# Seven block products for the value half of the up projections, on one Trainium2 core

## The chip, the core and the metric

The kernel runs on one core of one Trainium2 chip. The metric is the device time of the whole program in microseconds. Engines: PE (TensorE, matmul), PEld (its weight load), DVE (VectorE), ACT (ScalarE), POOL (GpSimd), SP (SyncE, which issues the loads; SPq is its queue). The SBUF and PSUM memories are shared by the engines; semaphores order them.

## What is computed

Two decoder layers for a prompt of 512 tokens and 8 x 8 sample tokens, 576 tokens in all, kept as `xT[128, 8, 576]` (features on partitions). Layer 0 mixes tokens with an mLSTM, layer 1 with sliding-window attention. Each is followed by the part that the change touches:

```
def conv_glu(h, conv_buf, w_up, conv_w, conv_b, w_down):   # h = rmsnorm(x)
    up = h @ w_up                     # 1024 -> 2 * 2816
    g, u = up[..., :D_FF], up[..., D_FF:]
    gp = jnp.concatenate([conv_buf, g], axis=1)
    gc = conv_b + sum(conv_w[j] * gp[:, j:j + T] for j in range(3))
    y = (gelu(gc) * u) @ w_down       # 2816 -> 1024
    return y, gp[:, T:]
```

`g` is called the gate half, `u` the value half. Weights are float32. Each is split into a high and a low float16 part; a product is three float16 matmuls (high x high, high x low, low x high; `THREE`).

## The kernel before

**Up projection** (`up0`, `up1`, one for each layer). 22 tiles of 128 outputs for either half, worked in pairs of tiles: pair i holds tiles i and i + 11. Its four units come in the order gate i, value i, gate i + 11, value i + 11. A unit is 8 k-blocks x 3 x 2 token halves of 288 (`HALF`) = 48 matmuls (`fm_unit`, L426), so a pair is 192. The weights pass through a ring of four slots: SP loads 512 KB into `stage` (`load`, L2234) once the DVE has read what was there; ACT writes the high part `wH` (`split_act`, L294), the DVE the low part `wL` (`split_dve`, L300), each once for each unit, and PE reads both. Behind each gate unit the DVE scales PSUM into `G` (L712), ACT and the DVE do the three taps of the convolution (L635, L716, L720) and ACT the gelu (L642); behind the value unit the DVE scales and multiplies (L729, L733). Sums of the quarters of the pair (L739 to L746, `tmix`) and their high and low parts (`hidH`, `hidL`, L647 to L651, L753 to L759) prepare the down projection. The order on each engine is written out by hand in `act_ffn` and `dve_ffn`, as a loop over i; only semaphores tie the engines together.

**Down projection** (`down0`, `down1`). It already uses a seven-product scheme (Winograd's form of Strassen's): for each of four pairs of output tiles the weight is cut into quarters A11, A12, A21, A22 (`quart`, 704 KB each), and seven products of sums of quarters with sums of hidden quarters replace eight. A product is 11 x 3 = 33 matmuls of 288 columns (L544), a pair 231, a layer 924. The sums of weights are made by the DVE (`weight_sum`, L365, L369) and by two adding DMAs on the POOL queue (`pool_sums`, `add_a22`, L377). The high part comes from ACT (`block_high`, L348), the low one from the DVE (`block_low`, L354). Each product goes to a PSUM bank of its own or adds to one; the DVE adds them into `xT` (`add_block`, L408).

## Time and profile before

| | us |
|---|---|
| median of 3 runs | 1230.67 (1230.65 to 1231.26) |
| the profiled execution, whole | 1233.18 |
| its span | 1231.4 |
| PE busy | 1212.6 (98%) |
| DVE busy | 808.1 (66%) |
| ACT busy | 536.9 (44%) |
| PE chain in one up projection after its first unit | 252.84 |
| PE chain in one down projection | 113.20 |

The profile is of one execution. The whole time is 1.8 us more than the span, and the profiled execution is 2.5 us above the median. A row of the timeline gives start, duration, engine, line and operands; durations of independent neighbours on one engine overlap a little, so starts can be closer than a duration.

### The profile page before, as it was taken

The page shows a single profiled execution, that of the slowest core. Times are in us where ns is not written, and L with a number is a line of the kernel's source. Part 1 is how long each engine was busy: PE and PEld are TensorE (multiplying, and loading weights), DVE is VectorE, ACT ScalarE, POOL GpSimd, SP SyncE. Part 2 cuts the span into 40 slices and gives each one's busy share as a digit, 9 for nine tenths or more (in the row PEclk, how much of TensorE's full clock was granted, in tenths as well). Part 3 has the DMA queues.
Part 4 walks back from the last instruction along what each step waited for, and adds up shares of the span by engine and source line. Part 5 has one row for each costly group of instructions (what it writes and reads, how often), then busy time and mean ns, then how long its engine had stood idle before and what let it go on. Part 6 is the DMA issues. An engine that isn't in the chain of part 4 may idle for free.

```text
span 1231.4 us, 24687 instructions
## 1 busy us (share of the span) xinstructions
PE 1212.6 (98%) x9846; PEld 921.9 (75%) x9846; DVE 808.1 (66%) x1309; ACT 536.9 (44%) x849; POOL 81.2 (7%) x227
## 2 busy tenths in 40 slices
PE   7999999999999999999999999999999999999998
PEld 6855777777777777777774456777777777778886
DVE  5644566566767767776763479755777677777564
ACT  6322355345434434443344459744344344333332
POOL 1000010000000000000003200000000000000010
PEclk9999999999999999999999999999999999999999
DMA  8642243233332232345646220022322323515672
GB/s 214 236 104 75 63 146 108 74 105 96 89 87 85 85 102 85 111 123 148 154 117 221 81 69 2 2 69 86 103 85 85 95 80 97 156 47 136 152 177 56
DMA packets 188830, 129.58 MB, mean 105 GB/s; under 512 B 4929, under 2 KB 177851, under 8 KB 188690
## 3 DMA queue, kind: packets, MB, share of 16 engines
q1 hardware_dynamic: 181562, 101.80, 28.6%
q0 software_dynamic: 7200, 26.80, 8.3%
q8 instruction: 51, 0.84, 0.3%
q14 instruction: 17, 0.14, 0.1%
HBM read 109.15 MB, written 9.86 MB: 97 GB/s over the span
## 4 chain that ended last, share of the span: by engine, by line
PE 94%; DVE 3%; SPq 1%; ACT 1%; DMA 1%; issue 0%; DVEq 0%
PE PS L426 57%; PE PS L544 18%; PE PS L442 10%; SPq L2234 1%; PE PS L1155 1%; PE PS L1175 1%; DMA rowsF<-in_ffn_conv_b 1%; PE PS L1130 1%; DVE P L2184 1%; DVE st L2165 1%; PE PS L1373 1%; PE PS L1406 1%; ACT P L1692 1%; PE PS L1229 0%; PE PS L1158 0%
## 5 line engine op out<-in xcount | busy, mean ns | idle before, releaser
L426 PE MATMUL PS<-zH,wH 128*128 128x288 f16 x1408 | 287.6, 286 | 0.0
L426 PE MATMUL PS<-zL,wH 128*128 128x288 f16 x1408 | 287.6, 286 | 0.0
L426 PE MATMUL PS<-zH,wL 128*128 128x288 f16 x1408 | 287.6, 286 | 0.0
L544 PE MATMUL PS<-hidH,blk 128*128 128x288 f16 x1232 | 227.9, 286 | 0.0
L300 DVE SCALAR_TENSOR_TENSOR wL<-stage,wH 128x1024 f16<-128x1024 f32 x140 | 170.3, 1219 | 56.9 <-ACT wH L294 56.9
L294 ACT ACTIVATE wH<-stage 128x1024 f16<-128x1024 f32 x140 | 146.4, 1048 | 131.7 <-PE PS L426 65.5
L544 PE MATMUL PS<-hidL,blk 128*128 128x288 f16 x616 | 176.2, 286 | 0.0
L426 PEld LDWEIGHTS PS<-zH,wH 128*128 128x128 f16 x1408 | 137.8, 98 | 35.0
L426 PEld LDWEIGHTS PS<-zL,wH 128*128 128x128 f16 x1408 | 137.8, 98 | 34.7
L426 PEld LDWEIGHTS PS<-zH,wL 128*128 128x128 f16 x1408 | 137.8, 98 | 34.7
L544 PEld LDWEIGHTS PS<-hidH,blk 128*128 128x128 f16 x1232 | 120.5, 98 | 30.2
L635 ACT ACTIVATE acc<-G,pff 128x592 f32<-128x592 f32 x44 | 38.7, 881 | 161.2 <-DVE G L712 161.2
L426 PE MATMUL PS<-hnH,wH 128*128 128x288 f16 x396 | 81.6, 288 | 1.8 <-issue 1.2
L426 PE MATMUL PS<-hnL,wH 128*128 128x288 f16 x396 | 81.7, 288 | 0.0
L426 PE MATMUL PS<-hnH,wL 128*128 128x288 f16 x396 | 81.5, 288 | 0.0
L712 DVE SCALAR_TENSOR_TENSOR G<-PS,three 128x288 f32<-128x288 f32 x132 | 39.0, 351 | 55.3 <-PE PS L426 46.0
L716 DVE SCALAR_TENSOR_TENSOR acc<-G,pff,acc 128x592 f32<-128x592 f32 x44 | 36.7, 835 | 55.9 <-ACT acc L635 55.9
L544 PEld LDWEIGHTS PS<-hidL,blk 128*128 128x128 f16 x616 | 60.3, 98 | 15.1
L354 DVE SCALAR_TENSOR_TENSOR blk<-quart,blk 128x1408 f16<-128x1408 f32 x32 | 51.7, 1617 | 25.5 <-ACT blk L348 25.5
L348 ACT ACTIVATE blk<-quart 128x1408 f16<-128x1408 f32 x32 | 43.0, 1368 | 52.2 <-DMA quart<-quart 34.2
L348 ACT ACTIVATE blk<-mixed 128x1408 f16<-128x1408 f32 x24 | 33.0, 1374 | 60.0 <-DVE mixed L365 37.8
L408 DVE SCALAR_TENSOR_TENSOR xT<-PS,xT 128x288 f32<-128x288 f32 (+1 forms) x56 | 30.2, 540 | 37.6 <-PE PS L544 37.6
(383 smaller groups left out, 1746.4 us busy)
## 6 DMA issues: line engine op xcount, KB each, us to landing
...
quart<-in_w_ffn_down SPq DMA_DIRECT2D x32, 704.0 KB, 5.0
...
quart<-quart POOLq DMA_DIRECT2D x8, 704.0 KB, 6.8
mixed<-quart POOLq DMA_DIRECT2D x8, 704.0 KB, 7.9
...
```

What stands on the lines that cost most here:

```text
L294: nc.scalar.activation(wH[:, slot, :], stage[:, slot, :], ACT.Copy, scale=WSCALE).then_inc(hi_ready, 1)
L300: nc.vector.scalar_tensor_tensor(out=wL[:, slot, :], in0=stage[:, slot, :], scalar=WSCALE, in1=wH[:, slot, :], op0=ALU.mult, op1=ALU.subtr ...
L348: nc.scalar.activation(blk[:, g % RING, 0, :], WEIGHT[j], ACT.Copy, scale=WSCALE).then_inc(hi_ready, 1)
L354: nc.vector.scalar_tensor_tensor(out=blk[:, g % RING, 1, :], in0=WEIGHT[g % BLOCKS], scalar=WSCALE, in1=blk[:, g % RING, 0, :], op0=ALU.mu ...
L408: nc.vector.scalar_tensor_tensor(out=x, in0=ps, scalar=1.0 / WSCALE, in1=x, op0=ALU.mult, op1=ALU.add).then_inc(added, 1)
L426: m = nc.tensor.matmul(out[:, hf, :], w[a][:, slot, 128 * (at + j):128 * (at + j + 1)], xs(b, k)[:, HALF * hf:HALF * (hf + 1)], start=(fir ...
L442: m = nc.tensor.matmul(out, x, w[:, cols], start=first, stop=last, skip_group_check=True)
L544: m = nc.tensor.matmul(down_bank(g), blk[:, g % RING, a, 128 * k:128 * (k + 1)], (hidH, hidL)[b][:, HIDDEN[j], k, :], start=(k == 0 and (a ...
L635: nc.scalar.activation(acc[:, s, 0:CC], G[:, s, 2:GC], ACT.Identity, bias=pff[:, k, 38 + L:39 + L], scale=pff[:, k, 32 + 3 * L + 2:33 + 3 ...
L712: last = nc.vector.scalar_tensor_tensor(out=out, in0=a, scalar=1.0 / WSCALE, in1=b, op0=ALU.mult, op1=ALU.mult)
L716: nc.vector.scalar_tensor_tensor(out=acc[:, s, 0:CC], in0=G[:, s, 0:CC], scalar=pff[:, k, 32 + 3 * L:33 + 3 * L], in1=acc[:, s, 0:CC], op0 ...
L1130: nc.tensor.matmul(PS[:, 4 + i % 2, 0:DV + 1], kw[:, i, 128 * h:128 * (h + 1)], vM[:, i, h, :], start=True, stop=True).then_inc(hsem["u"], 1)
```

## The change

**Up projection.** The first and the last pair (0 and 10) stay as they were. For pairs 1 to 9 the gate units stay, but the two value units become seven products of 4 x 3 = 12 matmuls of 288 columns (`product_of`), 84 where there were 96. The two tiles are the two output halves, k-blocks 0 to 3 and 4 to 7 the two input halves, the token halves the two column halves. Their weight tiles are v0 (tile i, slot 1 of `stage`) and v1 (tile i + 11, slot 3). The weight sums are made in place: S1 in slot 3 by an adding DMA of 256 KB (`step_s1`), N2 in slot 1 by the DVE (`up_n2`), then S4 and S3 in slot 1 by two more adding DMAs, one after the other (`step_s4`, `step_s3`, both in slot 1). The high and low parts of N2, S3 and S4 go to `sH` and `sL`. The sums of the inputs (`tH`, `tL`) are made once for each layer behind the mixer's output projection (`pair_scaled`, `t_sums`, `t_high`, `t_low`) and brought home by two DMAs. Four products of a pair gather in one PSUM bank; after each ACT copies the bank (`keep`: p1, u2, u3, c21) to `val`, and the DVE adds the other banks (`value`: c11, c22, c12). Gelu now writes into `h32`, and one DVE instruction multiplies (`hidden`). The loops and orders of all five queues in `pe_ffn`, `act_ffn`, `dve_ffn`, `pool_ffn` and the SP's `ffn` are rewritten; the peeled first and last steps included.

Units of a step on PE in order: u1, u2 (from v0), u3 (v1), u4 (N2), u5 (gate i, 48 matmuls), u6 (S3), half of gate i + 11, u7 (v1), u8 (S4), the other half (u9 is its end).

**Down projection.** Same count of products and matmuls, another order. Products 0, 2, 4 and 6 share one bank; ACT copies it after products 0, 2 and 4 (`keep_block`); the DVE combines in `val`, scales by `rstd` and adds (`combine_blocks`). One sum that a DMA made (into `mixed`) is now made by the DVE (`weight_s3`), one by a DMA (`pool_s4`).

Core of the diff (the deleted bodies of `two`, `weight_sum`, `pool_sums` and `add_block` can be seen above):

```diff
+        QUARTERS = ((A21, 1, 0), (A11, 0, 0), (A12, 0, 1), (A22, 1, 1))
+        N2_OF, S3_OF = 1, 2
+
+        WEIGHT = (quart[:, A11, :], quart[:, A12, :], mixed[:, :], quart[:, A21, :], quart[:, A11, :],
+                  quart[:, A12, :], quart[:, A22, :])
+        HIDDEN = (0, 2, 5, 3, 4, 1, 6)
+        BANK = (0, 3, 0, 2, 0, 1, 0)
+        OPENS = (0, 1, 3, 5)
...
+        def up_high(act, L, i, what):
+
+            j = i + 1
+            whole = what in ("g0", "g1") or (isinstance(j, int) and j == KH - 1)
+            first = isinstance(i, int) and i == 0
+            if what == "v1" and not whole:
+                act.wait_ge(s1_landed, up_s(L, j))
+            split_act(act, up_unit(L, j, what), up_base(L, i) + (SLOT[what] + 1 if first else FREED[what]),
+                      1 if whole else 2)
+
...
+        def s34_high(act, L, i):
+
+            j = i + 1
+            act.wait_ge(s3_landed, 16 * (len(MIXED) * L + j))
+            if not (isinstance(i, int) and i == 0):
+                act.wait_ge(unit_used, up_base(L, i) + FREED["s34"])
+            nc.scalar.activation(sH[:, WQ:3 * WQ], stage[:, 1, :], ACT.Copy, scale=WSCALE).then_inc(hi_ready, 2)
...
+        def s34_low(dve, L, j):
+
+            dve.wait_ge(hi_ready, up_base(L, j) + LOW["s34"])
+            nc.vector.scalar_tensor_tensor(out=sL[:, WQ:3 * WQ], in0=stage[:, 1, :], scalar=WSCALE,
+                                           in1=sH[:, WQ:3 * WQ], op0=ALU.mult, op1=ALU.subtract).then_inc(lo_ready, 2)
...
+        def up_n2(dve, L, j):
+
+            dve.wait_ge(s1_landed, up_s(L, j))
+            dve.wait_ge(lo_ready, up_base(L, j) + LOW["v0"])
+            nc.vector.tensor_tensor(stage[:, 1, 0:WQ], stage[:, 1, 0:WQ], stage[:, 3, 0:WQ],
+                                    ALU.subtract).then_inc(sums, 1)
...
+        def keep_block(act, L, g):
...
+            act.wait_ge(unit_used, block_num(L, g) + 1)
+            row, a = {0: (0, HALF), 2: (0, 0), 4: (1, 0)}[j]
+            nc.scalar.activation(val[row][:, a:a + HALF], down_bank(g), ACT.Copy).then_inc(ff["copied"], 1)
...
+        def combine_blocks(dve, L, g):
+
+            p, j = divmod(g, BLOCKS)
+            n0 = ADDS * L + PAIR_ADDS * p
+            last = p == PAIRS - 1
+            if j in (0, 2):
+                return
...
+            if j == 1:
+                dve.wait_ge(ff["copied"], kept(L, p) + 1)
+                sum_of(dve, v01, v01, b3, ALU.add, added)
+            elif j == 3:
+                dve.wait_ge(ff["copied"], kept(L, p) + 2)
+                sum_of(dve, v00, v00, b2, ALU.subtract, added)
+            elif j == 4:
+                dve.wait_ge(ff["copied"], kept(L, p) + 3)
+                sum_of(dve, v10, v10, b2, ALU.subtract, added)
+                dve.wait_ge(added, n0 + 3)
+                scale_row(dve, 0, HALF, 1)
+                if last:
+                    dve.wait_ge(added, n0 + 4)
+                    add_row(dve, 2 * p + 1, 0, HALF, 1)
+            elif j == 5:
+                n = n0 + (6 if last else 5)
+                dve.wait_ge(added, n0 + 2)
+                sum_of(dve, v00, v00, b1, ALU.add, added)
+                dve.wait_ge(added, n)
+                scale_row(dve, 0, T, 0)
+                dve.wait_ge(added, n + 1)
+                add_row(dve, 2 * p, 0, T, 0)
             else:
-                q = (0, 3, 3, None, 2, 0, 1)[j]
-                x = two[:, HALF * q:HALF * (q + 1)]
-            nc.vector.scalar_tensor_tensor(out=x, in0=ps, scalar=1.0 / WSCALE, in1=x, op0=ALU.mult,
...
+        def t_sums(dve, L, k):
...
+            n0 = 2 * (4 * L + k)
+            nc.vector.tensor_tensor(tt4[:, 0, :], zz[:, 0, :], zz[:, 1, :], ALU.subtract).then_inc(turned_x["t"], 1)
+            nc.vector.tensor_tensor(tt4[:, 1, :], zz[:, 2, :], zz[:, 0, :], ALU.subtract)
+            dve.wait_ge(turned_x["t"], n0 + 1)
+            nc.vector.tensor_tensor(tt4[:, 2, :], tt4[:, 0, :], zz[:, 2, :], ALU.subtract).then_inc(turned_x["t"], 1)
+            dve.wait_ge(turned_x["t"], n0 + 2)
+            nc.vector.tensor_tensor(tt4[:, 3, :], zz[:, 3, :], tt4[:, 2, :], ALU.add).then_inc(turned_x["sum"], 1)
...
+            def step(i):
+                n, vb, cb = up_base(L, i), VALS * L + 3 * i, COPIES * L + 4 * i - 2
+                pe.wait_ge(lo_ready, n + LOW["v0"])
+                pe.wait_ge(copied, cb)
+                product_of(v0, 0, x_quarter(0, 1), 0, True)
+                pe.wait_ge(vals, vb)
+                product_of(v0, WQ, x_quarter(1, 1), 3, True)
+                pe.wait_ge(lo_ready, n + LOW["v1"])
+                product_of(v1, 0, x_turned_pair(0), 2, True)
+                pe.wait_ge(copied, cb + 1)
+                product_of(of_sums, 0, x_turned_pair(2), 0, False)
+                pe.wait_ge(ff["gate"], KF * L + 2 * i + 1)
+                whole(i, 0, 0)
+                pe.wait_ge(lo_ready, n + LOW["s34"])
+                pe.wait_ge(copied, cb + 2)
+                product_of(of_sums, WQ, x_turned_pair(1), 0, False)
+                pe.wait_ge(ff["gate"], KF * L + 2 * i + 2)
+                whole(i, 1, 0, ks=range(KQ))
+                pe.wait_ge(copied, cb + 3)
+                product_of(v1, WQ, x_turned_pair(3), 0, False)
+                pe.wait_ge(vals, vb + 2)
+                product_of(of_sums, 2 * WQ, x_quarter(1, 0), 2, False)
+                whole(i, 1, 0, ks=range(KQ, KD))
+
...
+            def step_first(i):
+                keep(i, "p1")
+                up_high(act, L, i - 1, "g1")
+
+            def step_mid(i):
+                hidden_raw(i - 1)
+                keep(i, "u2")
+                hidden_turned(i - 1)
+                s34_high(act, L, i - 1)
+                tap(i, 0)
+                keep(i, "u3")
+
+            def step_last(i):
+                up_high(act, L, i, "v0")
+                gelu(i, 0)
+                n2_high(act, L, i)
+                keep(i, "c21")
+                up_high(act, L, i, "v1")
+                up_high(act, L, i, "g0")
...
+            def step_first(i):
+                value(i, "c11")
+                up_low(dve, L, i, "g1")
+                hidden(i - 1, 1)
+                turned(i - 1)
+                hidden_lows(i - 1)
+                s34_low(dve, L, i)
+                gate(i, 0)
+
+            def step_last(i):
+                up_low(dve, L, i + 1, "v0")
+                conv(i, 0)
+                value(i, "c22")
+                up_n2(dve, L, i + 1)
+                n2_low(dve, L, i + 1)
+                value(i, "c12")
+                up_low(dve, L, i + 1, "v1")
+                hidden(i, 0)
...
+            def step_s1(j):
+                pool.wait_ge(staged[3], (TURN0[f"up{L}"] + j + 1) * 16)
+                pool.dma_start(stage[:, 3, 0:WQ], stage[:, 3, WQ:2 * WQ], accum_op=ALU.add).then_inc(s1_landed, 16)
+
+            def step_s4(j):
+
+                pool.wait_ge(sums, up_sum(L, j))
+                pool.dma_start(stage[:, 1, WQ:2 * WQ], stage[:, 1, 0:WQ], accum_op=ALU.add).then_inc(s4_landed, 16)
+
+            def step_s3(j):
+
+                pool.wait_ge(s4_landed, up_s(L, j))
+                pool.wait_ge(lo_ready, up_base(L, j) + LOW["n2"])
+                pool.dma_start(stage[:, 1, 0:WQ], stage[:, 3, WQ:2 * WQ], accum_op=ALU.add).then_inc(s3_landed, 16)
+
...
+                    up_load(1, u)
+                for i in range(2, KH):
+                    for what in ("g0", "g1", "v1", "v0"):
+                        if what == "v1":
+                            sp.wait_ge(s3_landed, 16 * (len(MIXED) * L + i - 1))
+                            sp.wait_ge(lo_ready, up_base(L, i - 1) + LOW["v1"])
+                        else:
+                            sp.wait_ge(lo_ready, up_base(L, i - 1) + LOW["s34" if what == "v0" else what])
+                        up_load(i, SLOT[what])```

The DVE in the first layer's up projection, where a pair follows another. Before (one half of a loop pass; wL<-stage is `split_dve`, G<-PS the scaling of a gate unit, ntmp is `h32`):

```order
L720 SCALAR_TENSOR_TENSOR acc<-G,pff,acc 128x592
L299 REGISTER_ALU
L300 SCALAR_TENSOR_TENSOR wL<-stage,wH 128x1024 [waits hi_ready]
L727 REGISTER_ALU
L729 SCALAR_TENSOR_TENSOR ntmp<-PS,three 128x576 [waits ffn0_hL,unit_used]
L731 REGISTER_ALU
L733 TENSOR_TENSOR ntmp<-ntmp,acc 128x512 [waits ffn0_gelu,ffn0_u]
L734 TENSOR_TENSOR ntmp<-ntmp,acc 128x64
L739 TENSOR_TENSOR three<-ntmp 128x288 [waits ffn0_h32]
L299 REGISTER_ALU
L300 SCALAR_TENSOR_TENSOR wL<-stage,wH 128x1024 [waits hi_ready]
```

Now, from `s34_low(1)` to `hidden(1, 0)` (L466 is `s34_low`, L473 `up_n2`, L452 `n2_low`, L519 `value`, L1088 `hidden`):

```order
L466 SCALAR_TENSOR_TENSOR hidL<-stage,hidH 128x1024 [waits hi_ready]
L1058 SCALAR_TENSOR_TENSOR G<-PS,three 128x512 [waits unit_used,ffn_hist]
L1060 SCALAR_TENSOR_TENSOR G<-PS,three 128x8x8
L341 SCALAR_TENSOR_TENSOR wL<-stage,wH 128x1024 [waits hi_ready]
L1070 SCALAR_TENSOR_TENSOR acc<-G,pff,acc 128x592 [waits ffn_acc]
L1074 SCALAR_TENSOR_TENSOR acc<-G,pff,acc 128x592 [waits ffn_half]
L519 TENSOR_TENSOR C<-C,PS 128x288 [waits ffn_copied,unit_used]
L473 TENSOR_TENSOR stage<-stage 128x512 [waits lo_ready,s1_landed]
L452 SCALAR_TENSOR_TENSOR hidL<-stage,hidH 128x512 [waits hi_ready]
L519 TENSOR_TENSOR val<-val,PS 128x288 [waits unit_used]
L341 SCALAR_TENSOR_TENSOR wL<-stage,wH 128x1024 [waits hi_ready]
L1088 SCALAR_TENSOR_TENSOR ntmp<-val,ntmp 128x576 [waits ffn_gelu,ffn_vals]
```

What moved: the low part of the next pair's v0 (the first L341) now stands two instructions behind the read of slot 1 by L466, and the convolution, the sums and the multiplication of the pair stand behind it.

SP at the same place, before (one of four loads in a pass) and now (two pairs of tiles):

```order
L2234 ISA [waits lo_ready]
L2234 DMA stage<-in_w_ffn_up 128x8x128
L2233 REGISTER_ALU
L2234 ISA [waits lo_ready]
L2234 DMA stage<-in_w_ffn_up 128x8x128
```

```order
L2720 DMA stage<-in_w_ffn_up 128x8x128 [waits lo_ready] x6
L2720 DMA stage<-in_w_ffn_up 128x8x128 [waits lo_ready,s3_landed]
L2720 DMA stage<-in_w_ffn_up 128x8x128 [waits lo_ready] x3
L2720 DMA stage<-in_w_ffn_up 128x8x128 [waits lo_ready,s3_landed]
L2720 DMA stage<-in_w_ffn_up 128x8x128 [waits lo_ready] x3
```

What moved: before, each load waited for the low part of the unit that had its slot. Now the load of v0 comes last of its four and waits for the low parts of S3 and S4; that of v1 waits for the landing of S3.

ACT in pair 1, from the high part of S3 and S4 to that of pair 2's v1 (L335 is the high part of a tile, L447 that of N2, L461 that of S3 and S4, L942 `keep`, L908 the tap, L916 the gelu):

```order
L461 ACTIVATE hidH<-stage 128x1024 [waits s3_landed]
L908 ACTIVATE acc<-G,pff 128x592 [waits ffn_gate]
L942 ACTIVATE C<-PS 128x288 [waits unit_used,ffn_h32]
L335 ACTIVATE wH<-stage 128x1024 [waits unit_used,staged1]
L916 ACTIVATE ntmp<-acc 128x512 [waits hidden_low,ffn_conv]
L917 ACTIVATE ntmp<-acc 128x64
L447 ACTIVATE hidH<-stage 128x512 [waits unit_used,weight_sums]
L942 ACTIVATE C<-PS 128x288 [waits unit_used]
L335 ACTIVATE wH<-stage 128x1024 [waits staged3,unit_used,s1_landed]
```

What moved: before, taps, high parts, gelu and the copies to `hidH` alternated for each tile. Now the copies of PSUM banks stand among them, the high part of v0 stands ahead of the gelu, that of N2 behind it.

## Rows read from the trace of the kernel before

**Rows 1.** The page: span, and PE (busy us, share, instructions).
```profile
span 1231.4 us, 24687 instructions
PE 1212.6 (98%) x9846; PEld 921.9 (75%) x9846; DVE 808.1 (66%) x1309; ACT 536.9 (44%) x849; POOL 81.2 (7%) x227
```
**Rows 2.** The chain that ended last: start us, us, what; up0, down0.
```profile
283.43 252.84 PE PS L426 x2064
536.27 113.20 PE PS L544 x924
```
**Rows 3.** Windows: us, busy us (instructions) by engine, clock, DMA; up projection, attention.
```profile
380.00:403.50 23.50, 23.50 (x194) 18.77 (x193) 16.73 (x28) 9.43 (x12) 1.07 (x6) 1.00 0.31 89
727.00:760.00 33.00, 30.21 (x270) 20.23 (x269) 30.99 (x78) 29.55 (x105) 0.00 (x0) 1.00 0.01 4
```
**Rows 4.** Timeline of the DVE in up0: start us, us, instruction, idle before, releaser.
```profile
381.46 1.22 DVE L300 SCALAR_TENSOR_TENSOR wL<-stage,wH 128x1024 f16<-128x1024 f32 x1
...
391.51 0.83 DVE L716 SCALAR_TENSOR_TENSOR acc<-G,pff,acc 128x592 f32<-128x592 f32 x1 [1.32 <-ACT acc L635]
392.50 0.84 DVE L720 SCALAR_TENSOR_TENSOR acc<-G,pff,acc 128x592 f32<-128x592 f32 x1 [0.16 <-DVE acc L716]
...
395.98 0.69 DVE L733 TENSOR_TENSOR ntmp<-ntmp,acc 128x512 f32<-128x512 f32 x1
...
397.21 0.45 DVE L744 TENSOR_TENSOR three<-ntmp 128x288 f32<-128x288 f32 x1
...
399.09 0.75 DVE L756 TENSOR_TENSOR hidL<-ntmp,hidH 128x576 f32 x1
399.76 1.35 DVE L759 TENSOR_TENSOR hidL<-three,hidH 128x1152 f32 x1
401.06 0.89 DVE L712 SCALAR_TENSOR_TENSOR G<-PS,three 128x288 f32<-128x288 f32 x3
```
**Rows 5.** Timeline of ACT there.
```profile
385.18 0.44 ACT L647 ACTIVATE hidH<-ntmp 128x288 f32 x1 [0.69 <-DVE ntmp L734]
390.45 0.88 ACT L635 ACTIVATE acc<-G,pff 128x592 f32<-128x592 f32 x1 [4.83 <-DVE G L712]
391.23 1.04 ACT L294 ACTIVATE wH<-stage 128x1024 f16<-128x1024 f32 x1
393.37 0.70 ACT L642 ACTIVATE acc<-acc 128x592 f32<-128x592 f32 x1 [1.10 <-DVE acc L720]
...
398.16 1.16 ACT L651 ACTIVATE hidH<-three 128x1152 f32 x1 [0.55 <-DVE three L746]
```
**Rows 6.** Timeline of SP's queue there, and landing of `stage` loads, 380 to 430.
```profile
382.84 16.86 SPq L2234 DMA_DIRECT2D stage<-in_w_ffn_up  x4
DMA to landing us min/median/max: 3.6/3.7/4.2
```
**Rows 7.** DMA issues, whole run: out<-in, queue, count, KB each, median us to landing.
```profile
quart<-in_w_ffn_down SPq DMA_DIRECT2D x32, 704.0 KB, 5.0
quart<-quart POOLq DMA_DIRECT2D x8, 704.0 KB, 6.8
mixed<-quart POOLq DMA_DIRECT2D x8, 704.0 KB, 7.9
...
out_sample_k<-qtok POOLq DMA_DIRECT2D x8, 8.0 KB, 2.0
```
**Rows 8.** Timeline in down0: an adding DMA's issue, and the copy that waits for it.
```profile
617.30 0.86 POOL L377 DMA_DIRECT2D quart<-quart  x1 [24.62 <-DVE mixed L365]
622.65 1.38 ACT L348 ACTIVATE blk<-quart 128x1408 f16<-128x1408 f32 x1 [3.25 <-DMA quart<-quart]
```
**Rows 9.** Timeline of the DVE, last unit of the mixer's output projection.
```profile
276.73 0.76 DVE L474 SCALAR_TENSOR_TENSOR xT<-PS,xT 128x576 f32 x1 [1.43 <-PE PS L426]
278.55 0.82 DVE L487 SCALAR_TENSOR_TENSOR zL<-xT,pd,zH  x1 [1.07 <-ACT zH L480]
```
**Rows 10.** Timeline at the end, the last add into xT.
```profile
1226.49 0.46 DVE L408 SCALAR_TENSOR_TENSOR xT<-PS,xT 128x288 f32<-128x288 f32 x1 [4.13 <-PE PS L544]
```

More of the change, by code:

```diff
@@ L766, in dve_ffn @@
+            hidden_lows(i)
+            block_low(dve, L, 0)
+            weight_n2(dve, L, 0)
+            i = KH - 1
+            gate(i, 0)
+            conv(i, 0)
+            hidden(i, 0)
+            gate(i, 1)
+            conv(i, 1)
+            block_low(dve, L, 1)
+            hidden(i, 1)
+            turned(i)
+            hidden_lows(i)
+            block_work(dve, L, 2)
             if L == 0:
@@ L1488, in _ @@
             act.sem_inc(free["qkv"], TT)
[L1489 to L1490 removed]
+            act.sem_inc(ff["gate"], 2)
             act.wait_ge(dI, 16)
```

730 lines of the change are left out of this document (479 added, 251 removed).

## The prediction

> **What bounds the kernel now.** The page comes first: PE is busy 1212.6 of 1231.4 us [rows 1]. Then the chain of waits: each layer's up projection is one piece of PE without another engine in it, 2064 matmuls in 252.84 us, and the down projection 924 in 113.20 us [rows 2]. Both give 0.1225 us for a matmul of 288 columns. A pair of tiles takes 192 of them, 23.52 us; the window of a pair has PE busy throughout, the DVE for 16.73 and ACT for 9.43 of 23.50 us [rows 3]. So removed matmuls count in full as long as nobody becomes late, and the DVE has 6.8 us to spare in a pair. The timelines of the DVE and ACT then give the length of each step [rows 4, 5]: DVE 0.45 us for 288 columns, 0.69 for 512, 0.75 for 576, 1.22 for 1024, 1.35 for 1152; ACT 0.44 for 288, 1.04 for 1024, 1.16 for 1152. Independent neighbours start 0.08 us before the end of the one ahead; a DVE instruction that needs the one ahead starts 0.16 us behind its end.
>
> **Removed.** 9 pairs x 12 matmuls x 2 layers = 216, x 0.1225 = 26.5 us (13.2 a layer). A middle pair would take 180 x 0.1225 = 22.05 us. The down projection keeps its 924.
>
> **Added work in a middle pair.** DVE: the splits of S3, S4 (1.22) and N2 (0.69), N2 itself (0.69) and three additions (3 x 0.45); less in the multiplications. In order without any wait for another engine, with the same-engine waits of 0.16, its instructions from the low part of v0 to that of S3 and S4 take 18.0 us and the gate's 0.8 more: still below 22.05. By busy time alone it fits. ACT has some 13 us. What decides is the order and one slot of `stage`.
>
> **The loop through slot 1.** S3 and S4 of pair i stand in slot 1 until the DVE has read them (`s34_low`). Only then may SP load v0 of pair i + 1 there, and the DVE's next instruction but the gate's two is that tile's low part, with all else of the pair behind it. I follow one round, with 0 at the end of `s34_low(i)`:
> - SP issues 0.16 us later (the DVE ends at 382.68, the issue is at 382.84 [rows 4, 6]); landing after 3.7 [rows 6]: 3.9. ACT's high part 1.04: 4.95. The DVE can start the low part at 5.0; the 0.8 us of `gate(i, 0)` are over long before.
> - Low 1.22, two taps 0.83 and 0.84 with 0.16 between: 7.95. c22 8.3. N2 8.9. ACT's high part of 512 columns, not in the trace, lies between 0.44 and 0.70 us [rows 5]; I take 0.63: 9.6. Low 10.35. c12 10.7. ACT copies c21 and makes v1's high part: 10.9; low 12.15. `hidden(i, 0)` 12.85.
> - PE waits for c22 ahead of u8: 8.4. u8 and half a gate unit are 1.47 + 2.94, the last matmul and the start behind the wait some 0.25: u9 is done at 13.05, and with it `gate(i, 1)` can start. So both ways come to 13.05.
> - From there: gate 0.83, ACT's tap 0.88 with 0.26 ahead and 0.18 behind it, taps on the DVE end at 3.98, c11 4.35, g1's low 5.5, `hidden` 6.2, `turned` (576, 288, 288 columns, each behind the last) 8.3, low of three raw quarters 9.3, ACT's high part of the four sums ends 9.6, their low 10.95, `s34_low` 12.1.
> The round is 13.0 + 12.1 = 25.1 us, 3.05 above PE's own 22.05 and 1.6 above the pair of before. PE stands about 2.5 us ahead of u8 and 0.5 ahead of u6 in each. It does not shrink when PE waits, as PE is only one of its ways. Round one starts in step: `s34_low(1)` ends 0.4 us before PE wants it. Eight rounds follow (pairs 1 to 9): 8 x 3.05 - 0.4 = 24.0 us a layer.
>
> The bounds of a round: without any of the waits for ACT it is 18.0 + 5.1 = 23.1. Upwards, the load shares the DMA engines with S1 of the same pair, issued about then: 4.2, the longest of these loads [rows 6], to 5.0, that of 704 KB [rows 7], makes 25.6 to 26.4. I take 25.1, as the loads of before also had others close by.
>
> **The adding DMAs.** 256 KB is not in the trace: 2.0 us for 8 KB, 5.3 for 704 KB alone (617.30 to 622.65), medians of 6.8 and 7.9 beside loads [rows 7, 8]. I take 4, nearer to 704 KB's than its size. S4 and S3 one after the other have 13.5 us from N2 to `s34_high`, and with the load of v1 and S1 the whole ring closes up to 6.7 us each. So they are hidden, at a price of zero; the cover is gone above 6.7. The Trainium skill (DMA: Bandwidth & Descriptors, Anatomy of one DMA) states a fixed 2.0 us and bytes at 436 GB/s for this path, 2.6 us here; for 704 KB it would say 3.7, less than the 5.3 of the trace. By either the sums stay hidden.
>
> **Start of the up projection.** In the last four units of the mixer's projection the DVE gets `t_sums` (four of 0.45, two waits) and `t_low` (1.35) on top of 3.5 us; a unit is 5.88 and the DVE's part becomes 7.4 from the second on. It is 3.3 us late at the last. There zL came at 279.37 [rows 9], and its matmuls at 276.6 + 7 x 0.735 = 281.7: 2.3 us of cover. PE waits 1.0 us. Pair 9 has another order (g0 ahead of v0): c22 ends at 6.6 and u8 is 0.9 late.
>
> **Seam to the down projection.** Pair 10 gives PE 23.5 us of cover, but the DVE comes with a pair's debt. From `s34_low(9)` as 0: PE ends pair 10 at 34.4. The DVE: v0's low part 9.6, `gate(9, 1)` 11.4, lows of pair 9 25.8, `block_low(0)` (1.62 as in the trace's blocks) 27.3, `weight_n2` 29.8 (quarters landed by 22, their DMA sum by 28), `gate(10, 0)`, taps and `hidden` 35.9, `gate(10, 1)` and taps 39.8, `block_low(1)` 41.3, `hidden`, sums and lows 46.8, `block_low(2)` 48.3. PE waits for the value copy (0.9), for block 1 (2.4), for the last lows (1.7) and for block 2 (0.7): 5.7 us. Before, this place cost nothing [rows 2]. Bounds 2 and 10.
>
> **Down projection.** DVE work stays near 22 of 28.3 us a pair. The new dependence is A22, loaded last: `block_low(6)` ends at 18.3 of a pair, load 5.0, S1 5.3 to 6.8, N2 1.6, high 1.4, low 1.6: 33.6 to 35.1, wanted at 28.3 + 8.1 = 36.4. Bank copies have a whole product (4.04) each. Nothing. At each layer's end, the last block needs a scaling and an addition where one addition of 0.46 was [rows 10]: 0.6 us.
>
> **Sum** against the profiled execution: per layer -13.2 + 24.0 + 1.0 + 0.9 + 5.7 + 0.6 = +19.0. Two layers: +38. Span 1269, whole 1271; against the median 1230.67 it is 1268.7, rounded to 1268.
>
> **Rivals.**
> - *PE keeps its rate in the steps* (the load is early enough, or the DVE's steps overlap more than its timeline shows): -26.5 + 2 x (1.0 + 5.7 + 0.6) = -11.9, 1219 us. For it: DVE and ACT have the busy time. Against: the wait on slot 1 is a plain semaphore, and the low part stands first in an in-order queue. With the round at its lower bound of 23.1: 16 x 1.05 instead of 48 gives 1237. Faster than before is decided at a round below about 22.7.
> - *The adding DMAs close the ring* (6.7 us is the point): at 7.9 each, the median beside loads [rows 7], three of them add 3.6 us a round, 16 x 3.6 = 58: 1326. Against: a third of the bytes.
> - *The clock.* PE now stands 3 of 25 us. It kept its upper level, 2.4 GHz (granted 1.00), in the attention with 30.21 of 33.00 us busy [rows 3]. If it went to 1.2 GHz behind each wait for a quarter of a pair's matmuls, 5.5 us a round, it would be some 1356. The Trainium skill (TensorE: Matmul & The Clock Gate, Part 1) says that idling gates the clock; the attention's row speaks against it for gaps of this size.
>
> **Chances.** Forecast (1245 to 1290) 0.70; lower-bound round (about 1237) 0.10; PE at its rate (1219) 0.11; ring of DMAs or clock 0.09. A measurement can tell 0.2%, 2.5 us. Faster 0.12, same 0.03, slower 0.85. The range leaves out the 1219 and the upper rivals: 1235 to 1298.
>
> **What would show it.** The chain would no longer be PE alone in the up projections: loads of `stage`, ACT wH and DVE wL in it, starts of `s34_low` 25 us apart, 22 if I am wrong. PE idle ahead of u8 released by the DVE's c22, and ahead of block 1 at the seam. ACT's wait for `stage` slot 1 some 2 us a round. Wrong would be: a longer or shorter landing of the 512 KB load (16 rounds: 0.5 us is 8 us in all), adding DMAs above 6.7 us, or DVE instructions on `val` and `stage` that differ from rows of the same width.

## The result and the profile after

The changed kernel takes 1321.56 us (median of 4 runs, 1317.62 to 1322.12), the kernel before 1230.66 (4 runs, 1230.58 to 1231.26): a ratio of 1.0731, 95% interval 1.071 to 1.0752. It is slower, as forecast, but by 90.9 us where I had 38; the range ended at 1298. The profiled execution of the changed kernel took 1317.62 us in all, its span is 1315.8, 84.4 above the 1231.4 of before.

The page of the changed kernel, its first rows, the shares of the chain by engine, and the group of u8's first matmuls (section 5: busy us, mean ns of one, idle us ahead of them and what ended it):

```profile
span 1315.8 us, 24171 instructions
## 1 busy us (share of the span) xinstructions
PE 1216.3 (92%) x9630; PEld 907.9 (69%) x9630; DVE 864.7 (66%) x1299; ACT 615.1 (47%) x1035; POOL 150.1 (11%) x285
...
PE 53%; DVE 18%; ACT 9%; issue 9%; DMA 8%; SPq 1%; DVEq 1%; ACTq 0%; POOL 0%; POOLq 0%
...
L757 PE MATMUL PS<-zH,hidH 128*128 128x288 f16 x72 | 29.3, 407 | 50.7 <-DVE C L519 50.7
```

216 matmuls are gone (9846 to 9630), worth 26.5 us at 0.1225 each, and yet PE is busy 3.7 us longer than before [rows 1]. It stands idle 99.5 us of its span, where it stood 18.8. Half of that is one place: ahead of u8, until the DVE has made c22 (L519). And u8's matmuls, 286 ns each in the rest of the up projection, take 407 there.

The chain of waits of the changed kernel through one round (pair 3 to 4; start us, us, what), answering to [rows 2], in which such a round was PE alone:

```profile
396.02 1.23 DVE hidL L466
397.26 4.37 DMA stage<-in_w_ffn_up
401.79 1.06 ACT wH L335
402.95 0.11 DVE wL L341
...
405.83 0.46 DVE C L519
406.34 3.06 PE PS L757 x12
409.40 3.17 PE PS L601 x24
412.60 0.06 DVE G L1058
```

PE's idle time there and its first matmul of u8 and of u9 (timeline), then the granted clock around them (windows: us, busy us (instructions) for PE, PEld, DVE, ACT, POOL, then PE's clock, DMA share, GB/s), answering to [rows 3]:

```profile
406.34 0.42 PE L757 MATMUL PS<-zH,hidH 128*128 128x288 f16 x1 [3.00 <-DVE C L519]
...
412.39 0.29 PE L757 MATMUL PS<-zH,wH 128*128 128x288 f16 x1
```

```profile
396.02:423.25 27.23, 24.02 (x182) 18.17 (x181) 18.38 (x26) 12.06 (x18) 4.57 (x9) 0.94 0.44 106
404.00:406.00 2.00, 0.00 (x0) 0.00 (x0) 1.84 (x4) 0.05 (x1) 0.00 (x0) 1.00 0.00 0
406.00:408.00 2.00, 1.66 (x8) 1.04 (x9) 1.30 (x3) 1.81 (x5) 1.02 (x2) 0.57 0.00 0
408.00:410.00 2.00, 2.00 (x11) 1.33 (x10) 0.83 (x3) 1.74 (x2) 0.04 (x1) 0.57 0.72 131
```

The ring is the one of the forecast, link for link: `s34_low` (L466), the load of v0 into slot 1, ACT's high part, the DVE's low part, the taps, c22, u8, half a gate unit, `gate`. Its round is 27.3 us and not 25.1: `s34_low` starts at 315.57, 341.45, 368.74, 396.02, 423.25, 450.54, 477.84, 505.24 and 532.12 in layer 0, and 216.6 us apart from first to last in layer 1 too. Behind 3.00 us without a matmul the granted clock stands at 0.57, near the lower level of 1.2 GHz, and the 36 matmuls from u8 on take 6.05 us (406.34 to 412.39) instead of 4.42.

Three more places, PE's timeline at each (start of the up projections, layer 1's convolution rows, end of layer 0's down projection), then the chain ahead of the first and the adding DMAs of the whole run (DMA issues: count, KB each, median us to landing):

```profile
304.54 0.42 PE L757 MATMUL PS<-zH,wH 128*128 128x288 f16 x1 [6.09 <-ACT C L934]
919.00 0.42 PE L757 MATMUL PS<-zH,wH 128*128 128x288 f16 x1 [8.27 <-ACT C L934]
...
1190.01 2.03 PE L833 MATMUL PS<-C,convO 128*99 128x128 f32 x8 [7.27 <-POOL convO L1240]
...
688.07 0.39 PE L617 MATMUL PS<-wH,zH 128*128 128x512 f16 x1 [3.58 <-DVE wL L341]
```

```profile
287.41 0.53 POOL tL L1266
287.95 8.75 DMA stage<-stage
```

```profile
stage<-stage POOLq DMA_DIRECT2D x54, 256.0 KB, 3.2
```

### The profile page after: what moved, and what is told of

The parts are those of the page before. It is cut to its first block, busy times and chain, and to the rows that moved or that the text cites. A ratio compares the mean times of both kernels' runs of the same rounds, so it can differ in the third digit from the quotient of the medians.

```text
span 1315.8 us, 24171 instructions
## 1 busy us (share of the span) xinstructions
PE 1216.3 (92%) x9630; PEld 907.9 (69%) x9630; DVE 864.7 (66%) x1299; ACT 615.1 (47%) x1035; POOL 150.1 (11%) x285
## 3 DMA queue, kind: packets, MB, share of 16 engines
q0 software_dynamic: 15552, 45.68, 15.6%
## 4 chain that ended last, share of the span: by engine, by line
PE 53%; DVE 18%; ACT 9%; issue 9%; DMA 8%; SPq 1%; DVEq 1%; ACTq 0%; POOL 0%; POOLq 0%
PE PS L601 15%; PE PS L820 15%; PE PS L617 9%; PE PS L757 6%; DMA stage<-in_w_ffn_up 5%; DVE acc L1070 2%; ACT wH L335 2%; DVE wL L341 2%; DVE hidL L466 1%; DMA stage<-stage 1%; ACT acc L908 1%; ACT hidH L461 1%; DVE three L1097 1%; DVE ntmp L1088 1%; PE PS L1617 1%
## 5 line engine op out<-in xcount | busy, mean ns | idle before, releaser
L341 DVE SCALAR_TENSOR_TENSOR wL<-stage,wH 128x1024 f16<-128x1024 f32 x140 | 170.6, 1221 | 168.1 <-ACT wH L335 167.6
L335 ACT ACTIVATE wH<-stage 128x1024 f16<-128x1024 f32 x140 | 144.7, 1047 | 132.7 <-PE PS L617 58.8
L601 PE MATMUL PS<-zH,wH 128*128 128x288 f16 x832 | 171.7, 288 | 0.7 <-DVE zL L662 0.7
L601 PE MATMUL PS<-zL,wH 128*128 128x288 f16 x832 | 170.0, 286 | 0.0
L601 PE MATMUL PS<-zH,wL 128*128 128x288 f16 x832 | 169.9, 286 | 0.0
L908 ACT ACTIVATE acc<-G,pff 128x592 f32<-128x592 f32 x44 | 38.8, 881 | 128.9 <-DVE G L1060 128.9
L601 PEld LDWEIGHTS PS<-zH,wH 128*128 128x128 f16 x832 | 82.4, 99 | 23.6 <-DVE zL L662 1.3
L601 PEld LDWEIGHTS PS<-zL,wH 128*128 128x128 f16 x832 | 81.9, 98 | 21.3
L601 PEld LDWEIGHTS PS<-zH,wL 128*128 128x128 f16 x832 | 81.4, 98 | 20.5
L601 PE MATMUL PS<-hnH,wH 128*128 128x288 f16 x396 | 80.9, 286 | 1.8 <-issue 1.2
L601 PE MATMUL PS<-hnH,wL 128*128 128x288 f16 x396 | 80.8, 286 | 0.0
L601 PE MATMUL PS<-hnL,wH 128*128 128x288 f16 x396 | 80.8, 286 | 0.0
L412 DVE SCALAR_TENSOR_TENSOR blk<-quart,blk 128x1408 f16<-128x1408 f32 x48 | 77.5, 1618 | 0.8 <-ACT blk L406 0.7
L757 PE MATMUL PS<-zH,hidH 128*128 128x288 f16 x72 | 29.3, 407 | 50.7 <-DVE C L519 50.7
L916 ACT ACTIVATE ntmp<-acc 128x512 f32<-128x512 f32 x44 | 27.8, 631 | 89.0 <-DVE acc L1074 89.0
L519 DVE TENSOR_TENSOR val<-val,PS 128x288 f32<-128x288 f32 x60 | 27.1, 451 | 55.9 <-PE PS L820 29.6
L757 PE MATMUL PS<-zH,wH 128*128 128x288 f16 x144 | 42.4, 295 | 14.4 <-ACT C L934 14.4
## 6 DMA issues: line engine op xcount, KB each, us to landing
quart<-in_w_ffn_down SPq DMA_DIRECT2D x32, 704.0 KB, 5.6
stage<-stage POOLq DMA_DIRECT2D x54, 256.0 KB, 3.2
quart<-quart POOLq DMA_DIRECT2D x8, 704.0 KB, 5.7
quart<-mixed POOLq DMA_DIRECT2D x8, 704.0 KB, 5.3
```

What stands on the lines that cost most here:

```text
L335: nc.scalar.activation(wH[:, slot, :], stage[:, slot, :], ACT.Copy, scale=WSCALE).then_inc(hi_ready, inc)
L341: nc.vector.scalar_tensor_tensor(out=wL[:, slot, :], in0=stage[:, slot, :], scalar=WSCALE, in1=wH[:, slot, :], op0=ALU.mult, op1=ALU.subtr ...
L412: nc.vector.scalar_tensor_tensor(out=blk[:, g % RING, 1, :], in0=WEIGHT[g % BLOCKS], scalar=WSCALE, in1=blk[:, g % RING, 0, :], op0=ALU.mu ...
L519: nc.vector.tensor_tensor(out, a, b, op).then_inc(done, 1)
L601: m = nc.tensor.matmul(out[:, hf, :], w[a][:, slot, 128 * (at + j):128 * (at + j + 1)], xs(b, k)[:, HALF * hf:HALF * (hf + 1)], start=(fir ...
L757: m = nc.tensor.matmul(up_psum(bank), w[a][:, at + 128 * k:at + 128 * (k + 1)], x(b, k), start=(start and k == 0 and (a, b) == THREE[0]), ...
```

## The experiments

The theory after the result, **A**: PE waits for the ring through slot 1, and what the forecast lacked is (1) some 0.6 us more for load and issue, (2) the low clock behind the wait, 1.6 us a round, and (3) two things that GpSimd's queue holds back. The rivals: **B**, the adding DMAs set the round; **C**, the matmuls of u8 are slow for a reason of their own.

### e1_conv_first: c22 ahead of the low part of v0

```diff
@@ ACT, step_last(i)
-                up_high(act, L, i, "v0")
                 gelu(i, 0)
+                up_high(act, L, i, "v0")
...
@@ DVE, step_last(i)
-                up_low(dve, L, i + 1, "v0")
                 conv(i, 0)
                 value(i, "c22")
+                up_low(dve, L, i + 1, "v0")
```

> In the last third of a middle round DVE makes the conv and the copy c22 before the low half of v0's split, and ACT makes gelu(i,0) before its high half; nothing else changes. Theory A (the loop through slot 1, made dearer by TensorE's clock): c22 is then there at about 4.4 us after s34_low instead of 9.0, before TensorE comes to u8 at about 5.9, so the 3.0 us wait ahead of u8 goes, its 12 matmuls take 1.47 us again instead of 3.06, and a round falls from 27.3 to 23.1 to 23.4 us: 16 rounds by 4, about -60 us, time 1255 to 1265. Rival B (the adding DMAs of the quarter sums or their queue on GpSimd set the round): the round stays at 27.0 to 27.5 us and only the place of the wait moves, time 1310 to 1325. Rival C (the wait goes but the low clock has another cause, such as the load of the whole program): round 24.8 to 25.4, time 1280 to 1295.

Measured: 1263.53 us (1260.16 to 1264.98), 1.0261 of before (1.0232 to 1.029). Rounds of 23.4 to 23.9, most 23.43. The DVE's timeline of a round, and u8's group:

```profile
387.12 1.22 DVE L466 SCALAR_TENSOR_TENSOR hidL<-stage,hidH 128x1024 f16<-128x1024 f32 x1
...
391.35 0.83 DVE L1074 SCALAR_TENSOR_TENSOR acc<-G,pff,acc 128x592 f32<-128x592 f32 x1 [0.16 <-DVE acc L1070]
392.10 0.45 DVE L519 TENSOR_TENSOR C<-C,PS 128x288 f32<-128x288 f32 x1
394.06 1.22 DVE L341 SCALAR_TENSOR_TENSOR wL<-stage,wH 128x1024 f16<-128x1024 f32 x1 [1.50 <-ACT wH L335]
```

```profile
L757 PE MATMUL PS<-zH,hidH 128*128 128x288 f16 x72 | 20.6, 286 | 0.7 <-DVE C L519 0.7
```

c22 now ends 4.2 us after `s34_low` and not 9.0, 50.0 of the 50.7 us of idle time ahead of u8 are gone and its matmuls are back at 286 ns. The rounds of both layers, first to last `s34_low`, fell by 28.0 us each: 56 of the 58 us. B and C fall. No work was taken away: only the places of the high and the low part of v0 changed, which now stand behind the gelu on ACT and behind the two taps and c22 on the DVE. But a ring is left, and 23.43 is hardly less than before's 23.52 a pair: PE now waits 1.2 to 1.7 us for `s34_low` in 14 of the rounds. The chain still goes through the load (388.36, 4.19 us), the low part of v0 and all that stands behind it.

### e2b_fill: the waiting time filled with matmuls

```diff
@@ PE, step(i)
                 product_of(v1, WQ, x_turned_pair(3), 0, False)
+                for _ in range(28):
+                    nc.tensor.matmul(PS[:, 1, HALF:512], zH[:, 1, 0:128], zH[:, 0, 0:512 - HALF], start=True, stop=True,
+                                     skip_group_check=True)
                 pe.wait_ge(vals, vb + 2)
```

> TensorE runs 28 matmuls of 224 columns into columns of bank 1 that nobody reads, right ahead of its wait for the copy c22 in every middle pair; they are no part of the computation. By 95 ns each (the rate of the unit matmuls around them at the full clock) they fill 2.66 of the 3.0 us that TensorE stands idle there. Theory A (the idle time lowers TensorE's clock, and the low clock makes u8 3.06 us instead of 1.47): u8 takes about 1.5 us again though the work ahead of it has grown, the round falls from 27.3 to 25.4 to 25.8 us, time 1291 to 1298. Rival B (the clock falls for another reason, for instance by a limit on power): u8 stays near 3 us, the round at 27.3 or above, time 1318 to 1326. Rival C (the 12 matmuls of u8 are slow by what they read or by the bank they write, with the clock only following): u8 stays near 3 us with a granted clock of 1 in its stretch, time 1318 to 1322.

Measured: 1302.94 us (1299.88 to 1303.38), 1.0575 of before (1.0556 to 1.0593): 18.6 us faster than the changed kernel, with 504 matmuls more. PE's timeline at the same place, and the windows:

```profile
402.51 2.85 PE L792 MATMUL PS<-zH 128*128 128x224 f16 x28
405.36 0.30 PE L757 MATMUL PS<-zH,hidH 128*128 128x288 f16 x1
...
409.78 0.29 PE L757 MATMUL PS<-zH,wH 128*128 128x288 f16 x1
```

```profile
404.00:406.00 2.00, 2.00 (x21) 1.62 (x19) 1.80 (x3) 0.84 (x3) 0.20 (x1) 1.00 0.00 0
406.00:408.00 2.00, 2.00 (x19) 1.60 (x17) 1.14 (x3) 2.00 (x4) 0.86 (x1) 1.00 0.22 40
```

The 36 matmuls from u8 on take 4.42 us, the clock is 1.00, and the round is 25.3 to 26.2. So the idle time lowers the clock, and 1.6 us of each slow round is the clock. The time is 5 us above what A gave. A took 1.5 to 1.9 us off all 16 rounds; together they became 21.9 us shorter, and the first of each layer no shorter at all (25.91 and 25.93 us, they were 25.88 and 25.81), since its wait had not lowered the clock. Of the other 3.3 us the profile shows 2.4 ahead of any filling: the 36 matmuls behind the wait at the start of the up projections took 6.60 and 7.25 us, where the changed kernel's took 5.76 and 5.73. `s34_low(1)` of layer 0 starts at 317.61, not 315.57.

### e3_half_load: half of v0's load

```diff
@@ SP, the load of v0 in pairs 2 to 9
+                        if what == "v0" and i < KH - 1:
+                            sp.dma_start(stage[:, 1, 0:WQ]..., tile(i, 1)[:, 0:KQ, :]).then_inc(staged[1], 16)
+                        else:
+                            up_load(i, SLOT[what])
```

> The load of v0 in the middle pairs fetches four of its eight k-blocks, 256 KB instead of 512 KB; half of v0 is left out of the computation and what stands in slot 1 from before is used in its place. Everything else, the order included, is as in the changed kernel. Theory A (the load's landing is a link of the ring s34_low, load, split of v0, c22, u8, gate, s34_low): the load lands 1.0 to 1.8 us earlier than its 4.4 us, and each round is shorter by that and by up to 1.6 us more where the shorter wait ahead of u8 no longer lowers the clock: round 24 to 26.3 us, time 1265 to 1306. Rival B (the ring closes elsewhere, by the adding DMAs on the GpSimd queue): round 27.0 to 27.5, time 1312 to 1324.

Measured: 1292.05 us (1290.76 to 1294.32), 1.0492 of before (1.0468 to 1.0516), 29.5 us less than the changed kernel. The load's piece in the chain is 3.17 us (at 393.88) and not 4.37, so c22 comes 1.2 us earlier; over the 16 rounds the median is 3.57 us where it was 4.57. The rounds now are of two kinds: 24.4 to 25.0 and 26.1 to 26.7. Two of them, PE's first matmul of u8 in each, then two windows of each:

```profile
401.76 0.30 PE L757 MATMUL PS<-zH,hidH 128*128 128x288 f16 x1 [1.79 <-DVE C L519]
...
426.67 0.30 PE L757 MATMUL PS<-zH,hidH 128*128 128x288 f16 x1 [2.30 <-DVE C L519]
```

```profile
402.00:404.00 2.00, 2.00 (x19) 1.59 (x17) 1.30 (x3) 1.81 (x4) 0.86 (x1) 1.00 0.00 0
404.00:406.00 2.00, 2.00 (x19) 1.61 (x17) 1.74 (x3) 1.15 (x2) 0.00 (x0) 1.00 0.72 131
...
426.00:428.00 2.00, 1.33 (x11) 1.07 (x12) 1.30 (x4) 1.54 (x4) 0.69 (x2) 0.97 0.00 0
428.00:430.00 2.00, 2.00 (x10) 1.25 (x9) 1.83 (x3) 2.00 (x3) 0.37 (x1) 0.50 0.61 112
```

The load is on the ring with its full length, and the step between the two kinds is the clock. Of the run's 16 waits ahead of u8 in pairs 1 to 8, the eight up to 1.94 us all have 36 matmuls at full pace behind them (4.42 us); of the eight from 2.14 to 2.45, six have slow ones (5.98 to 6.09).

### e4_pool_order: two moves on GpSimd

```diff
@@ POOL
             history(0, 1)
+            step_s1(1)
             pool.wait_ge(unit_used, SEG0[f"up{L}"])
             for home, new, ready in ((tH, newTH, turned_x["high"]), (tL, newTL, turned_x["low"])):
...
-            step_s1(1)
             tails(0, 0)
...
             pool_s1(pool, L, 0)
-            pool_s4(pool, L, 0)
             tails(KH - 1, 0)
             tails(KH - 1, 1)
+            pool_s4(pool, L, 0)
```

> Two moves in GpSimd's order and nothing else: the sums for pair 1 are issued ahead of the two copies of tH and tL to their home (1.18 MB each), and the two tails of the last row ahead of the second adding DMA of down product 0. Theory (I did not see in the forecast that what is queued ahead on GpSimd delays the start of the up projections and the seam of layer 1): the idle time of TensorE ahead of step 1 (6.1 us in layer 0, 8.3 us in layer 1) falls to under 1.5 us, with it the low clock of u1 and u2 right behind it (1.5 us a layer), and the 7.3 us that TensorE waits in layer 1 for the rows of the convolution falls to under 1.5 us; about -20 us, time 1298 to 1305. Rival (the sums of pair 1 are late by their own loads, and the seam waits for the down weights): both waits stay within 2 us of what they were, time 1312 to 1322.

Measured: 1305.22 us (1303.87 to 1307.85), 1.0609 of before (1.0582 to 1.0636): 16.3 us less than the changed kernel, just short of the 17 to 24 that I had. The 7.27 us wait for the convolution's rows is gone, with 1.50 at the next place. At the start only part went:

```profile
302.28 0.30 PE L757 MATMUL PS<-zH,wH 128*128 128x288 f16 x1 [3.60 <-ACT C L934]
```

3.60 in both layers, not under 1.5. The rest is ACT's own order: the copy of the value bank (L934) stands behind the gelu and a high part. e8 takes that up.

### e5_own_slot: the load taken out of the ring

```diff
+        stageX = sb("stageX", [128, 1024], into=ph)     # over rows 8 and 9 of hidL
...
+        def v0slot(j):
+            return stageX[:, :] if j in (2, 4, 6, 8) else stage[:, 1, :]
...
@@ SP, ahead of the four loads of pair i
+                    if i < KH - 1:
+                        sp.wait_ge(lo_ready, up_base(L, i - 1) + LOW["v0"])
+                        sp.dma_start(v0slot(i)..., tile(i, 1)).then_inc(stagedX if i in (2, 4, 6, 8) else staged[1], 16)
```

> v0 of pairs 2, 4, 6 and 8 has a buffer of its own in rows of the hidden tensor that are not written yet, pairs 3, 5, 7 and 9 keep slot 1; SyncE issues v0's load first in each round, and no longer after s34_low of the same round but after v0's low half of the round before. The order on DVE and ACT is that of the changed kernel. Theory A (the ring goes through the load of slot 1, 4.4 of the 9.0 us from s34_low to c22): with the load long landed, ACT's high half follows s34_low's neighbours at once, c22 is there before or within 0.5 us of TensorE's coming to u8 (5.9 us after s34_low), the clock stays at 1 and the round is 22.1 to 23.3 us, time 1237 to 1258. Rival B (the ring closes by the adding DMAs of the quarter sums, whose slot is the same): the sums now wait for a slot that is free earlier, so nothing of it should be seen; were their own time the limit, the round would stay at 26.5 to 27.5 us, time 1308 to 1324.

Measured: 1254.73 us (1252.28 to 1258.88), 1.019 of before (1.016 to 1.022). But for the first of each layer (23.5 and 23.4) the rounds are 22.80 us, to 0.01. The chain from 380 to 403 is PE for 97.8% of the time, and PE waits 0.58 us for c22. With the instructions in the changed kernel's own order, the ring is gone once the load need not wait for `s34_low`. The adding DMAs are the same 54, so B is out here too.

The edit has one thing more, which I had not named: as the buffer alternates, the middle passes of ACT and the DVE, a loop in the changed kernel, are written out in e5, e6 and e8. That has a price of its own. The changed kernel has both forms in one trace. From `gate(i, 1)` to the end of `s34_low` the same instructions take 11.87 us in a loop pass (412.60 to 424.47) and 11.25 us behind the loop, where the last pass is written out:

```profile
522.09 0.69 DVE L1058 SCALAR_TENSOR_TENSOR G<-PS,three 128x512 f32<-128x512 f32 x1 [0.77 <-PE PS L601]
...
532.12 1.22 DVE L466 SCALAR_TENSOR_TENSOR hidL<-stage,hidH 128x1024 f16<-128x1024 f32 x1
```

In e1 and e7 it is 11.88 in the loop too; in e5, e6 and e8 it is 11.24 in every round. So up to 0.6 of the 4.5 us that a round lost here can be the loop and not the slot; no run tells the two apart.

### e7_conv_pool and e6_both: the cures together

e7 is e1 with e4. e6 is e1, e4 and e5.

> Both cures together: conv and c22 ahead of v0's low half (with gelu ahead of its high half), and the two moves in GpSimd's order. Theory A (the three losses lie one behind another in time, so what each cure gains adds up): 1321.6 less 58.0 less 16.3, about 1247, range 1243 to 1252. Rival (they overlap, as the late start of the up projections would be absorbed by the wait of a later round): 1255 to 1262. Either way it is slower than the kernel before, 1230.7, by what the rounds still lose against TensorE's own rate and by the end of the down part.

Measured: 1248.99 us (1247.6 to 1255.01), 1.0161 of before (1.0132 to 1.019). Theory A's sum of the two gains holds within 2 us.

> All three cures: the own buffer for v0 of every other pair with its load issued a round early, conv and c22 ahead of v0's low half, and the two moves on GpSimd. Theory A (what is left of the round after conv and c22 go first is the ring through the load of slot 1): the round is TensorE's own 22.1 to 22.6 us instead of about 23.5, 16 rounds by 1.1 less than with the two other cures alone, time 1226 to 1238: between 0.5% faster and 0.5% slower than before. Rival (the ring of gate, hidden, split s34 and the copies on DVE and ACT sets 23.2 us by itself): time 1244 to 1250.

Measured: 1230.93 us (10 runs, 1228.61 to 1234.95), 1.0005 of before (0.9992 to 1.0019): the same time. The run of 1228.61 us has a mean granted clock of 0.998, that of 1234.95 one of 0.991. Rounds of 22.33 to 22.69 behind a first one of 23.5, against 22.05 for PE's own. So the loss of 90.9 us came from the order, one shared slot, the waits that follow from them and, for up to 9 us (14 passes by 0.64), the loops, and not from the products. The time and the round are as theory A had them, but its cause is not shown alone: a round fell by 1.0 us from e7 to e6, and 0.6 of it can be the loop. And the gain? In the profiled runs PE is busy 22.1 us less than before, but idle 36.8 instead of 18.8. The rows of e6 that stand for most of it, the start (3.60, in both layers), the seam, and the end of layer 0:

```profile
302.33 0.30 PE L785 MATMUL PS<-zH,wH 128*128 128x288 f16 x1 [3.60 <-ACT C L962]
...
536.93 0.30 PE L848 MATMUL PS<-hidH,blk 128*128 128x288 f16 x1 [1.18 <-DVE hidL L1137]
538.55 0.28 PE L848 MATMUL PS<-hidH,blk 128*128 128x288 f16 x1 [0.72 <-DVE blk L420]
...
1113.23 0.30 PE L848 MATMUL PS<-hidH,blk 128*128 128x288 f16 x1 [1.50 <-ACT val L574]
...
647.63 0.39 PE L645 MATMUL PS<-wH,zH 128*128 128x512 f16 x1 [3.58 <-DVE wL L349]
```

### e8_ends: the start and the end

e6 with two more moves.

```diff
@@ ACT, start of an up projection
             tap(0, 1)
+            value(0, 1)
+            up_high(act, L, 0, "v1")
             gelu(0, 1)
-            up_high(act, L, 0, "v1")
-            value(0, 1)
...
@@ DVE, end of layer 0's down projection
+                if L == 0 and g == PAIRS * BLOCKS - 1:
+                    split_dve(dve, unit("qkv", 0, 0))
                 combine_blocks(dve, L, g)
...
-                split_dve(dve, unit("qkv", 0, 0))
                 norm_tile(2 * PAIRS - 1)
```

> The kernel with the own buffer for v0, conv and c22 first and GpSimd's two moves, and two more moves at the places where its trace still has TensorE idle: at the start of each up projection ACT copies the value bank and makes v1's high half ahead of the gelu of row (0, 1) (TensorE waits there 3.60 us in each layer), and at the end of layer 0's down projection the DVE makes the low half of the next projection's first unit ahead of the last combination instead of behind it and a norm tile (TensorE waits there 3.58 us). Theory A (these waits are on the path, as what stands ahead of the copies and of the split has nothing to do with them): 3.60 becomes 0.5 to 1.2 twice and 3.58 becomes 0 to 0.5, so 8 to 9.5 us less than 1230.9: 1221 to 1224, 0.5 to 0.8% faster than the kernel before. Rival (the rounds that follow take the debt: the ring of DVE and ACT in pair 1 starts no earlier, and TensorE waits as much ahead of the sums of pair 1 or 2 instead): 1226 to 1229.

Measured: 1219.23 us (1218.27 to 1220.74), **0.991 of before** (0.9893 to 0.9926). This version is faster than both: by 11.4 us, 0.9% and clear of the scatter, than the kernel before, and by 102.3 than the changed one. The busy times on its page, and PE's waits that are left at the two starts (timeline):

```profile
PE 1189.5 (98%) x9630; PEld 897.8 (74%) x9630; DVE 865.1 (71%) x1299; ACT 614.4 (50%) x1035; POOL 145.5 (12%) x285
```

```profile
298.91 0.30 PE L785 MATMUL PS<-zH,wH 128*128 128x288 f16 x1 [0.74 <-ACT C L962]
...
865.71 0.29 PE L785 MATMUL PS<-zH,wH 128*128 128x288 f16 x1 [1.14 <-DMA tL<-hidH]
```

In layer 1 PE now waits for one of the copies that e4 put behind the sums of pair 1; it costs 1.14 us. The wait at the end of layer 0 is gone. The gain is 11.7 us where A gave 8 to 9.5. The idle rows account for 8.9; the profiled spans differ by 9.8, and the rest lies in the scatter of e6's ten runs.

## Why the prediction was right, and where it was wrong

**What bounds before, and what is removed: right.** A middle pair of 180 matmuls takes 22.33 us in e8 (421.79 to 444.12) with PE busy for 22.07 of them, where 22.05 was forecast. Over the whole run PE is busy 23.1 us less than before and not 26.5. That e8's 1219.23 us meets the 1219 of the rival *PE keeps its rate* is in part luck. This price had 14.6 us of waits in it, at the start, the seam and the end of both layers; e8 has 1.9 us of waits at the starts and 3.4 at the seams, and its 16 rounds are together 7.8 us above 22.05 each.

**The loop through slot 1: right in mechanism, wrong in size.** All links were named in their order, and the second half of a round (from the gate's start behind u9 to the end of the next `s34_low`) was given as 12.05 us and measured as 11.87 (412.60 to 424.47). That is close partly by luck: 0.6 us of it is the loop (see e5), which the sum did not have. In the first half, with 0 at the end of `s34_low`, here 397.24:

| step | forecast | measured |
|---|---|---|
| v0 landed | 3.9 | 4.4 |
| low part of v0 starts | 5.0 | 5.7 |
| c22 done | 8.3 | 9.0 |
| u8 starts | 8.4 | 9.1 |
| u9 done, `gate(i, 1)` starts | 13.05 | 15.36 |
| the round | 25.1 | 27.2 |

The term *landing 3.7* was 4.37 in this round and 4.57 in the median of the 16: 0.7 to 0.9 us a round. The sum of S1 is issued beside it, as the text said when it set 4.2 to 5.0 as upper bound; of the round's other three loads two landed in 3.6 us (387.34 and 390.86), and the third, issued 0.5 us behind one of them, in 4.68; S1 itself took 3.84 us (396.29), where the two other sums took 3.2. I took 3.7 because the loads of before had others close by too. The term *1.47 + 2.94* for u8 and the half unit was 3.06 + 3.17: the low clock, 1.6 us in this round by the starts of the first and the 37th matmul. Together the rounds of a layer are 15.8 us longer than 8 x 25.1.

**The clock: the failed step.** I had it as a rival, at 5.5 us a round, and gave it, with the DMA ring, 0.09. What I argued against it was an average, 30.21 of 33.00 us busy in the attention [rows 3], held against 3 of 25 idle in a round. But the idle time of a round lies in one piece of some 3 us, and the longest wait of the attention, up to the first unit behind it, is 1.18 us. In the changed kernel seven pairs of each layer pay (pairs 2 to 8, whose waits are 2.82 to 3.45 us; pair 1's, of 2.48 and 2.39, was followed by full pace): 1.3 to 1.65 us each above 4.42, 20.7 us in all. So the step that failed is the sum's nothing for the clock: the rival's price of 5.5 us was all or nothing, and what came was a small price that 14 of 16 rounds paid. The direction was forecast rightly; the time lies above the range by 23.6 us. The Trainium skill (TensorE: Matmul & The Clock Gate, Part 1) says that idling gates the clock. The trace of after agrees in these rounds, 0.57 behind 3.00 us idle.

**The adding DMAs: right.** 256 KB landed in 3.2 us in the median of 54, I took 4; they are hidden, and e1, e5 and e6 shorten the round with all of them in place.

**The start: missed.** I had 1.0 us, for late zL, and that was right in kind (0.43 and 0.24 us). Not in the sum was that GpSimd starts two copies of 1.18 MB ahead of S1 of pair 1, whose landing then takes 8.75 us in the chain (10.85 in layer 1), holds N2, and with it ACT, where `n2_high` stands ahead of the tap, the gelu and the copy that PE waits for. PE waits 6.09 and 8.27 us, and again runs at the lower clock behind it: 6.8 and 8.8 us more than forecast. e4 shows that the copies ahead of S1 are part of it: without them both waits are 3.60 us. The diff shows the order. I had costed each queue's instructions for the DVE, ACT and SP, and not walked through GpSimd's.

**The seam: half right in layer 0, missed in layer 1.** Layer 0 has 1.18 us for the last lows and 0.72 for block 2: 1.9 where I had 5.7. There was none for the value copy or for block 1. Further in, at 607.51, PE waits 0.39 us for a copy of a bank, which was forecast to cost nothing. In layer 1 PE waits 7.27 us for the rows that GpSimd copies (`tails` of the last row), as these stand behind an adding DMA that waits for the low part of block 1. The forecast took both layers as equal and did not look at who else stands in that queue.

**The end of layer 0: 0.6 forecast, 1.9 measured** (3.58 idle for 1.69 before), as the split of the next unit stands behind two instructions more and a norm tile. The rest of the down projection is at PE's rate, as said: PE is busy 114.03 of its 116.42 us in layer 0, and was 113.36 of 113.36.

**The account.** By the profiled spans the changed kernel is 84.4 us above before and the forecast had 38, so 46.4 us are to be explained. The rounds give 31.6 (20.7 of them the clock), the starts 15.6, the seams and the bank copy -1.8, the end of layer 0 1.3: 46.7 in all.

**The rivals.** The round's lower bound, 23.1, was thought to give 1237. e1 came near to that round, 23.43, and is at 1263.5, 26.5 us above: 14.5 us are what the two moves on GpSimd give back (e7, 1249.0), and 7.5 are its 16 rounds, 377.1 us where 16 x 23.1 is 369.6. The point from which the change pays was put at a round below 22.7. e5 misses it by 0.1 and is slower; e6 has 22.6 in the mean and only the same time; e8 has 22.5 and gains. The 11.7 us between e6 and e8 lie outside the rounds, so the point holds only roughly.
